# A one-hot gate matrix built eight tokens at a time instead of four

## The reference, cut to what matters

```python
e1 = jnp.take_along_axis(i1, pos // PEER_TOPK, axis=-1)
e2 = jnp.take_along_axis(i2, pos % PEER_TOPK, axis=-1)
idx = e1 * N_KEYS + e2
gate = jax.nn.softmax(best, axis=-1)
u_sel = expert_u[idx]
act = jax.nn.gelu(jnp.einsum('bqhkd,bqd->bqhk', u_sel, xb).astype(jnp.float32), approximate=False)
w = (gate * act).astype(xb.dtype)
return jnp.einsum('bqhk,bqhkd->bqd', w, expert_v[idx])
```

## Time and profile before

| What | us |
|---|---|
| median of 3 runs | 1726.26 |
| lowest and highest run | 1724.62, 1731.73 |
| the profiled execution, its own time | 1727.33 |
| its span in the trace | 1725.0 |

### The profile page before, as it was taken

The page is one execution under the profiler, slowest core; times in us unless marked ns, Lnnn a source line. Parts: engine busy times, 40 slices in busy tenths (PEclk is TensorE's granted clock), DMA queues, the critical chain, the costliest instruction groups (busy, mean ns, idle before and its releaser), DMA issues.

```text
span 1725.0 us, 20488 instructions
## 1 busy us (share of the span) xinstructions
PE 1622.8 (94%) x6590; PEld 1159.5 (67%) x6590; DVE 1184.2 (69%) x2625; ACT 342.8 (20%) x783; POOL 883.3 (51%) x1117
## 2 busy tenths in 40 slices
PE   7989999999899989987799999999999999999997
PEld 5768887686687658876366666666666666666664
DVE  4656488569664559799766766766666666667666
ACT  3244331212343112388000000001000000000001
POOL 6756566348653337600745544545654455445442
PEclk9999999999999989999899999999999999999999
DMA  6422235344897964200999999999999999999997
GB/s 211 122 74 74 68 122 153 113 156 135 295 323 273 352 219 135 85 0 9 399 409 409 409 409 409 409 409 409 408 409 403 408 409 408 409 409 407 409 408 270
DMA packets 139100, 489.47 MB, mean 284 GB/s; under 512 B 16497, under 2 KB 17009, under 8 KB 138881
## 3 DMA queue, kind: packets, MB, share of 16 engines
q0 software_dynamic: 73728, 268.47, 39.7%
q1 hardware_dynamic: 65280, 219.85, 35.0%
HBM read 483.53 MB, written 4.72 MB: 283 GB/s over the span
## 4 chain that ended last, share of the span: by engine, by line
DMA 40%; PE 33%; DVE 12%; POOL 7%; issue 5%; ACT 2%; SPq 1%; DVEq 0%; POOLq 0%; ACTq 0%
DMA ring<-in_expert_v,chosen 23%; DMA ring<-in_expert_rows,chosen 16%; PE pair L723 15%; PE pair L735 4%; POOL ring L692 4%; DVE ring L1476 4%; DVE ring L1473 3%; PE pair L1029 2%; PE pair L770 1%; DVE temp L1712 1%; PE pair L756 1%; PE pair L1013 1%; PE pair L816 1%; PE pair L793 1%; PE pair L971 1%
## 5 line engine op out<-in xcount | busy, mean ns | idle before, releaser
L692 POOL DMA_INDIRECT ring<-in_expert_rows,chosen x256 | 286.5, 1119 | 359.8 <-DVE ring L1473 320.2
L1013 PE MATMUL pair<-temp,hnT 128*128 128x512 f32 x984 | 445.5, 595 | 25.8 <-DVE hnT L1352 21.8
L1476 DVE SCALAR_TENSOR_TENSOR ring<-ring,chosen 128x1024 f32<-128x1024 f32 x256 | 328.9, 1285 | 156.6 <-DMA ring<-in_expert_v,chosen 154.0
L1004 PE MATMUL pair<-hnT,temp 128*128 128x256 f32 x1904 | 430.4, 379 | 0.0
L1004 PEld LDWEIGHTS pair<-hnT,temp 128*128 128x128 f32 x1904 | 361.8, 190 | 100.0 <-issue 56.9
L1473 DVE SCALAR_TENSOR_TENSOR ring<-ring 128x1024 f32<-128x1024 f32 x256 | 311.1, 1224 | 131.2 <-DMA ring<-in_expert_rows,chosen 130.0
L692 POOL DMA_INDIRECT ring<-in_expert_v,chosen x256 | 266.7, 1042 | 251.2 <-DVE ring L1476 230.1
L1013 PEld LDWEIGHTS pair<-temp,hnT 128*128 128x128 f32 x984 | 182.9, 190 | 224.5 <-issue 213.8
L1326 ACT ACTIVATE hnT<-pair 128x256 f32<-128x256 f32 x119 | 45.7, 384 | 811.7 <-PE pair L1004 685.1
L723 PE MATMUL pair<-hnT,gate_all 128*128 128x256 f32 x592 | 135.3, 385 | 1.4 <-issue 1.4
L723 PEld LDWEIGHTS pair<-hnT,gate_all 128*128 128x128 f32 x592 | 112.6, 194 | 16.5 <-issue 1.7
(11 more groups left out here) (292 smaller groups left out, 1925.0 us busy)
## 6 DMA issues: line engine op xcount, KB each, us to landing
temp<-in_expert_v SPq DMA_DIRECT2D x128, 512.0 KB
temp<-in_expert_u SPq DMA_DIRECT2D x119, 512.0 KB
gate_all<-in_w_query SPq DMA_DIRECT2D x27, 512.0 KB
ring<-in_w_g SPq DMA_DIRECT2D x16, 512.0 KB, 3.5
gate_all<-in_w_g SPq DMA_DIRECT2D x11, 512.0 KB
gate_all<-in_expert_u SPq DMA_DIRECT2D x9, 512.0 KB
ring<-in_w_u SPq DMA_DIRECT2D x8, 512.0 KB, 4.1
ring<-in_w_k SPq DMA_DIRECT2D x8, 512.0 KB, 4.0
```

The lines of the kernel that those rows point to most:

```text
L692: pool.indirect_dma_start(out=gathered[:, g % SLOTS, :], out_offset=None, in_=(expert_rows, expert_v_rows)[part], in_offset=bass.IndirectO ...
L1004: mm = pe.matmul(u_out[n % 2], u_in[:, n % 2, c * P:(c + 1) * P], hnT[:, c, FIRST[1]:L], start=(c == 0), stop=(c == DC - 1))
L1013: mm = pe.matmul(pairs[i][:, b * 512:(b + 1) * 512], weighed[n][:, i * P:(i + 1) * P], v_in[:, n % 2, b * 512:(b + 1) * 512], start=False, ...
L1476: dve.scalar_tensor_tensor(out=fin, in0=slot, scalar=wsel[:, at:at + 1], in1=fin, op0=ALU.mult, op1=ALU.add).then_inc(row_done, 1)
```

## The change

Groups now hold eight tokens, so there are 32 of them, two to a turn of the loop (still 16 turns). Both one-hot matrices begin as a bf16 comparison of 128x1024 on VectorE, the second key's and then the first key's, each into a single `marks` buffer of its own with the eight tokens inside. ScalarE widens the second key's marks to float32 (128x1024), reading with a step of eight bf16 elements (16 bytes). VectorE makes `oh1` with one float32 product of 128x1024: the first key's marks, read with the same step of 16 bytes, times the gates, repeated along the keys. This product waits on a semaphore for the comparison just ahead of it on its own engine. TensorE does eight matmuls a group, and ScalarE copies 128x1024 to G. `oh1` and `oh2` have two buffers each in place of four, PSUM two pairs of banks in place of four banks. `numbers` has 1024 elements and moves to its own buffer, shared with `q_head` and `y_odd`; the two lists of keys are both bf16. ScalarE widens one group ahead in place of two.

```diff
@@ -207,10 +207,11 @@
         one_head = sb("one_head", [P, HEADS], BF16)
-        q_head = sb("q_head", [P, 2, P])
-        y_odd = sb("y_odd", [P, HALF])
+        head_or_numbers = sb("head_or_numbers", [P, 2, HALF])
+        q_head = head_or_numbers[:, 0, :].rearrange("p (a b) -> p a b", a=2)
+        y_odd = head_or_numbers[:, 1, :]
         gathered = ring[:, 0:SLOTS, :]
@@ -218,19 +219,17 @@
         act = [hnT[:, b, 0:HALF] for b in range(2)]
-        marks = [hnT[:, 4 + b, 0:HALF].bitcast(BF16).rearrange("p (e t) -> p e t", t=4) for b in range(2)]
-        numbers = hnT[:, 6, 0:HALF].bitcast(BF16).rearrange("p (e t) -> p e t", t=4)
-        gate_sel = hnT[:, 7, 0:HALF]
+        marks = [hnT[:, 4 + 2 * a:6 + 2 * a, 0:HALF].bitcast(BF16).rearrange("p a (e t) -> p a e t", t=8) for a in range(2)]
+        numbers = head_or_numbers[:].rearrange("p a b -> p (a b)").bitcast(BF16).rearrange("p (a e t) -> p a e t", a=2, t=8)
         spare = [cd[:].rearrange("p a b c -> p (a b c)")[:, b * HALF:(b + 1) * HALF] for b in range(4)]
         wsel = chosen[:, 0, HALF:SEQ]
-        first_key = chosen[:, 1, 0:HALF]
-        second_key = chosen[:, 1, HALF:HALF + HALF // 2].bitcast(BF16)
+        both_keys = chosen[:, 1, 0:HALF].bitcast(BF16).rearrange("p (a t) -> p a t", a=2)
+        gate_sel = chosen[:, 1, HALF:SEQ]
         gate_chosen = chosen[:, 2, 0:HALF]
-        oh1 = v_in.rearrange("p s (b t e) -> p (s b) t e", b=2, t=4)
-        oh2 = [u_in[:, s, b * 512:(b + 1) * 512].rearrange("p (t e) -> p t e", t=4) for s in range(2) for b in range(2)]
+        oh1, oh2 = (v.rearrange("p s (t e) -> p s t e", t=8) for v in (v_in, u_in))
@@ -265,7 +264,7 @@
         ncum_parts = region(O_NCUM, L // 2).bitcast(BF16)
-        y_hold = [region(O_NCUM + L // 2, HALF), y_odd[:, :]]
+        y_hold = [region(O_NCUM + L // 2, HALF), y_odd]
         second_part = fgate[0:HEADS, 0, 0:L // 2].bitcast(BF16)
@@ -356,8 +355,8 @@
         numbers_ready = sem("numbers_ready")
-        oh2_marked, oh1_ready, oh2_ready, onehot_free, gmat_free = (
-            sem("oh2_marked"), sem("oh1_ready"), sem("oh2_ready"), sem("onehot_free"), sem("gmat_free"))
+        first_marked, second_marked, oh1_ready, oh2_ready, onehot_free, gmat_free = (
+            sem("first_marked"), sem("second_marked"), sem("oh1_ready"), sem("oh2_ready"), sem("onehot_free"), sem("gmat_free"))
         sel_gelu, row_done = sem("sel_gelu"), sem("row_done")
@@ -519,7 +518,7 @@
-            sp.wait_ge(onehot_free, 4 + HALF // 4)
+            sp.wait_ge(onehot_free, 2 + HALF // 8)
             load_v(0)
@@ -977,7 +976,7 @@
-            pe.sem_inc(onehot_free, 4)
+            pe.sem_inc(onehot_free, 2)
             pe.wait_ge(chosen_ready, 1)
@@ -1020,17 +1019,16 @@
             with pe.Fori(0, HALF // 16) as it:
-                for s in range(4):
-                    g = it * 4 + s
+                for s in range(2):
+                    g = it * 2 + s
                     pe.wait_ge(gmat_free, g + 1)
-                    pe.wait_ge(oh2_ready, g + 3)
-                    pe.wait_ge(oh1_ready, g + 1)
-                    for t in range(4):
-                        mm = pe.matmul(pairs[2 + s // 2][:, (s % 2) * 512 + t * P:(s % 2) * 512 + (t + 1) * P],
-                                       oh2[s][:, t], oh1[:, s, t], start=True, stop=True)
+                    pe.wait_ge(oh2_ready, g + 2)
+                    pe.wait_ge(oh1_ready, g + 2)
+                    for t in range(8):
+                        mm = pe.matmul(pairs[2 + s][:, t * P:(t + 1) * P], oh2[:, s, t], oh1[:, s, t], start=True, stop=True)
                     mm.then_inc(onehot_free, 1)
-            pe.wait_ge(gmat_free, 4 + HALF // 4)
+            pe.wait_ge(gmat_free, 2 + HALF // 8)
             for n in range(P):
@@ -1271,8 +1269,8 @@
             queries(1)
-            ac.sem_inc(gmat_free, 4)
-            ac.sem_inc(oh2_ready, 2)
+            ac.sem_inc(gmat_free, 2)
+            ac.sem_inc(oh2_ready, 1)
             def gelu_ahead(n):
@@ -1287,33 +1285,31 @@
             ac.sem_inc(gelu_done, AHEAD)
-            ac.activation(numbers, iota[:].unsqueeze(2).to_broadcast([P, P, 4]), ACT.Copy).then_inc(numbers_ready, 1)
-            evac(("idx", 0), first_key, (0, HALF))
-            evac(("idx", 1), second_key, (0, HALF))
+            ac.activation(numbers.rearrange("p a e t -> p (a e) t"), iota[:].unsqueeze(2).to_broadcast([P, P, 8]), ACT.Copy).then_inc(numbers_ready, 1)
+            for a in range(2):
+                evac(("idx", a), both_keys[:, a, :], (0, HALF))
             evac(("idx", 2), gate_chosen, (0, HALF))
             def widen(g, b):
-                ac.wait_ge(oh2_marked, g + 1)
+                ac.wait_ge(second_marked, g + 1)
                 ac.wait_ge(onehot_free, g + 1)
-                ac.activation(oh2[b], marks[b % 2].rearrange("p e t -> p t e"), ACT.Copy).then_inc(oh2_ready, 1)
+                ac.activation(oh2[:, b].rearrange("p t (a e) -> p t a e", a=2), marks[1].rearrange("p a e t -> p t a e"),
+                              ACT.Copy).then_inc(oh2_ready, 1)
             def read_gates(g, b, place):
-                ac.wait_ge(onehot_free, g + 5)
-                ac.activation(G[:, :, place],
-                              pairs[2 + b // 2][:, (b % 2) * 512:(b % 2 + 1) * 512].rearrange("p (t e) -> p e t", t=4),
-                              ACT.Copy).then_inc(gmat_free, 1)
+                ac.wait_ge(onehot_free, g + 3)
+                ac.activation(G[:, :, place], pairs[2 + b].rearrange("p (t e) -> p e t", t=8), ACT.Copy).then_inc(gmat_free, 1)
             widen(0, 0)
-            widen(1, 1)
             with ac.Fori(0, HALF // 16 - 1) as it:
-                for b in range(4):
-                    widen(it * 4 + b + 2, (b + 2) % 4)
-                    read_gates(it * 4 + b, b, bass.ds(it * 16 + b * 4, 4))
-            for b in range(4):
-                g = HALF // 4 - 4 + b
-                if b < 2:
-                    widen(g + 2, b + 2)
-                read_gates(g, b, slice(4 * g, 4 * g + 4))
+                for b in range(2):
+                    widen(it * 2 + b + 1, (b + 1) % 2)
+                    read_gates(it * 2 + b, b, bass.ds(it * 16 + b * 8, 8))
+            for b in range(2):
+                g = HALF // 8 - 2 + b
+                if b == 0:
+                    widen(g + 1, 1)
+                read_gates(g, b, slice(8 * g, 8 * g + 8))
@@ -1354,7 +1350,7 @@
             dve.memset(vm, 0.0)
-            chain(dve.memset(q_head[:], 0.0))
+            chain(dve.memset(q_head, 0.0))
             dve.wait_ge(dve_consts, 1)
@@ -1699,19 +1695,20 @@
             dve.wait_ge(numbers_ready, 1)
+            dve.sem_inc(oh1_ready, 1)
+            every = [P, 2, P // 2, 8]
             with dve.Fori(0, HALF // 16) as it:
-                for b in range(4):
-                    g = it * 4 + b
-                    dve.wait_ge(oh2_ready, g + 1)
-                    key = second_key[:, bass.ds(it * 16 + b * 4, 4)].unsqueeze(1)
-                    dve.tensor_tensor(marks[b % 2], numbers, key.to_broadcast([P, P, 4]), ALU.is_equal)\
-                       .then_inc(oh2_marked, 1)
+                for b in range(2):
+                    g = it * 2 + b
+                    tokens = bass.ds(it * 16 + b * 8, 8)
+                    for a, free, marked in ((1, oh2_ready, second_marked), (0, oh1_ready, first_marked)):
+                        dve.wait_ge(free, g + 1)
+                        dve.tensor_tensor(marks[a], numbers, both_keys[:, a, tokens].unsqueeze(1).unsqueeze(1).to_broadcast(every),
+                                          ALU.is_equal).then_inc(marked, 1)
+                    dve.wait_ge(first_marked, g + 1)
                     dve.wait_ge(onehot_free, g + 1)
-                    for t in range(4):
-                        at = it * 16 + b * 4 + t
-                        ins = dve.tensor_scalar(oh1[:, b, t], iota[:], first_key[:, bass.ds(at, 1)],
-                                                gate_chosen[:, bass.ds(at, 1)], ALU.is_equal, ALU.mult)
-                    ins.then_inc(oh1_ready, 1)
+                    mul(oh1[:, b].rearrange("p t (a e) -> p t a e", a=2), marks[0].rearrange("p a e t -> p t a e"),
+                        gate_chosen[:, tokens].unsqueeze(2).unsqueeze(2).to_broadcast([P, 8, 2, P // 2])).then_inc(oh1_ready, 1)
@@ -1723,7 +1720,7 @@
-            dve.wait_ge(gmat_free, 4 + HALF // 4)
+            dve.wait_ge(gmat_free, 2 + HALF // 8)
             for n in range(P):
```

## The result

The changed kernel took 1750.81 us as the median of four runs (1748.29 to 1753.80), the kernel before 1726.42, of four as well. The ratio is 1.0137, with a 95% interval from 1.0108 to 1.0165: slower by some 24 us, where 18.5 were forecast (1745).

A forecast was written before the change was run, and what follows sets the result against it. VectorE was taken to bound the 89 us stage: 3.24 us per eight tokens against 2.72 gives +16.7 us over 32 groups, and the stage's ends +1.8, so +18.5 us and 1745 us; range 1720 to 1762.

The forecast's parts named there:

- One to one: Transfers after the stage wait for its end, so a change of its length should reach the kernel's end in full.
- this sign of being wrong: The prediction is wrong if the loop after the stage, about 908 us, changes its length by more than 2 us.
- The comparisons: VectorE's two bf16 comparisons of 1024 elements in each group, forecast near 0.68 us each.
- C: Rival: the comparisons lose their pairing, each taking 0.53 us more, 34 us in all, about 1779 with the step; chance 0.05.
- The product's step: VectorE's product reads marks 16 bytes apart, priced like a 64-byte step: 0.68 us more for 1024 elements, 1.90 in all.
- A: Rival: the 16-byte step is free, product 1.15 us to the next start, loop -5.1 us, kernel 1723 us; chance 0.28.
- The dearer price that the prediction quotes: The skill's 2.50 ns a column on VectorE for a small step of 24 words, giving some 1771 us.
- The wait: VectorE's gap between second comparison and the product that needs it: 0.12 us, ends 0.03 and 0.5.
- The period: VectorE's time for eight tokens in the stage's loop: 3.24 us against 2.72, +16.7 us over 32 groups.
- TensorE's clock: In the stage TensorE would be busy 65% of the period; elsewhere, 68% busy, it kept 2.4 GHz.
- D: Rival: TensorE's clock falls to 1.2 GHz, sixteen records take about 4 us and set the period, 1755 to 1770; chance 0.04.

The follow-up runs named there:

- step32: The changed kernel with both readers' step doubled from 16 to 32 bytes, values in another order; 1744.30 us in one run.
- widen_seq: The changed kernel, but only ScalarE's widening reads its marks one after another, the product keeping its 16-byte step; 1748.45 us, ratio 1.0126.
- both_seq: The changed kernel, but product and widening both read the marks one after another, values in another order; 1724.42 us, ratio 0.9982.
- no_self_wait: The changed kernel, but the product reads the constant key numbers and needs no wait for the comparison ahead; 1741.91 us, ratio 1.0090.
- split: The changed kernel with 8-byte steps, second comparison and widening cut into halves of four tokens, one half-comparison between first comparison and product; 1717.19 us, ratio 0.9942.
- pair_across: The changed kernel reading marks in pairs 8 bytes apart, the product's pairs across 16-byte borders, the widening's within; 1745.38 us in one run.

## Why the prediction was right, and what it mis-sized

- **One to one.** Every stage's length reached the end: from the first load of `v` to the end pass 908.2 us before and 908.2 to 910.1 in the eleven experiments, whose stages differ by 30 us. The changed kernel's profiled execution has 911.2. I had put 2 us as the mark at which the prediction would be wrong here, so this sign of being wrong came up. 0.4 us are the longer last copy, which the forecast had. Most of the rest goes with TensorE's clock in the 62 us behind the first load, which before and in the changed kernel read (columns as in the earlier trace rows):

```profile
816.81:878.81 62.00, 49.99 (x128) 25.25 (x129) 46.09 (x81) 1.36 (x3) 43.10 (x35) 0.92 1.00 391
838.87:900.87 62.00, 47.40 (x101) 22.25 (x102) 45.07 (x80) 1.41 (x2) 39.04 (x33) 0.83 0.98 377
```

  The granted clock was 0.83 in place of 0.92, and 377 GB/s moved in place of 391. That leaves 0.87 MB over, which at the 408 GB/s of the following stretch is 2.1 us (an estimate from these rows). It is not the stage's length that does it: step32, with the same instructions and a stage of 108.3 us against the changed kernel's 109.7, had 0.97 and 394 GB/s there and passed 908.3 us to the end; widen_seq, with 109.0 us, had 0.94, 393 GB/s and 909.5 us. Over the thirteen traces the time behind the load grows with the time that TensorE spent there at 1.2 GHz (correlation 0.82 of the two times). Whether the clock is the cause, and why it fell more in this execution, no run here tests.
- **The comparisons** kept their pairing (C falls), at 0.68 us.
- **The product's step** was the right mechanism at the wrong size. "I take the price of 64 bytes": 0.67 ns an element from line 1630, 1.90 us in all. It was 0.78 us for 1024 elements, 2.00 us in all, which is 3.2 us over 32 groups. A reduction was a fair witness for the kind of cost, 13% short in its amount. A falls: by the prediction it needed 1.36 us or less. By its own rows and ends that point is 1.32 us (2.72 - 1.8/32 - 0.61 - 0.68 - 0.12, and 0.07 of overlap). Where the step was taken away, in both_seq, A's sum came true: 1724.42 us against its 1723. The dearer price that the prediction quotes, with 1771 us, did not come either.
- **The wait:** 0.12 us forecast, 0.14 measured, 0.6 us in all.
- **The period:** 3.36 us against 3.24, so 107.5 us against 103.7 for the loop. From the first comparison to the first load that came to +21.1 us where the sum has +17.7. With the begin (+0.9 against +0.44, as the write of `numbers` itself began 0.5 us later) and the 3.0 us behind the load, of which the sum had 0.4, this makes up the 6.6 us between the forecast's +18.5 and the traces' +25.1; between the medians it is 6 us. That the median came within 6 us is thus the step's right mechanism, not luck, but nearly half of the miss is nothing the prediction names. Its "about 106 us" for the stage up to the last copy's end was too low by its own sum (89.1 + 16.7 + 1.4 = 107.2); it took 110.7.
- **ScalarE** was taken as 1.74 us for the widening on VectorE's price for the step. It pays 1.0 us for 1024 elements, not 0.68. It stayed under VectorE all the same, by some 0.4 us, as its pause shows.
- **TensorE's clock** kept its level: granted 0.97 over the stage against 0.98, with the matmuls busy 61% of it, and no period was set by TensorE. It was at 1.2 GHz for 6.8 us at the stage's beginning, against 3.4 us before. D falls for the stage; the clock fell behind it, as said above.

## What to carry to other kernels

When a layout interleaves items so that a later reader has to step through it, look at the step in bytes: two reads in a row should share an aligned stretch of 16 bytes. Here that meant four bf16 items inside and not eight. Where the items are more than that, cut the buffer in halves of four rather than widen the interleave. A bigger instruction saves fixed cost only if its rate stays; and where an engine must wait for its own result, put an independent instruction between, since that hid 0.22 us in each of 32 groups and left a gain of 0.16 after the cost of the extra instruction.

## What the runs showed of the hardware

- A read that pays costs nearly the same time on both engines: 2.00 us on VectorE and 2.07 on ScalarE for 1024 bf16 elements, whether at 16 or at 32 bytes. VectorE loses 0.78 us by it, ScalarE 1.02.
- A step of 8 bytes is free on VectorE (1225 against 1225 ns in both_seq) and costs ScalarE 1147 against 1050 ns (both_seq); in aligned pairs 64 bytes apart ScalarE needs 1110.
- A wait on VectorE's own result costs 0.04 us of gap and 0.08 us of lost overlap (step32, no_self_wait), an address that changes with the turn 0.10 more behind such a wait, and all of it vanishes if one independent instruction of 0.42 us is in progress (split).
- In the 62 us behind the first load, a granted clock of 0.83 went with 377 GB/s (changed), 0.86 with 383 and 388 (both_seq, pair_across), and 0.92 to 0.97 with 388 to 394 (seven kernels); which of the two is the cause was not tested.
